# Hybrid encoder block: the softmax sums of the last four latent heads taken over by GpSimd additions

## The reference

```python
s = jnp.einsum('bqhd,bkhd->bhqk', q_blk, k).astype(jnp.float32) * scale
prob = jax.nn.softmax(s, axis=-1)
return jnp.einsum('bhqk,bkhd->bqhd', prob.astype(v.dtype), v)
```

## Time and profile before

| | us |
|---|---|
| median of 3 runs (lowest, highest) | 1581.14 (1579.66, 1581.53) |
| profiled execution: its own time | 1581.29 |
| its span in the profile | 1579.4 |
| PE busy | 1525.7 (97%) |
| DVE busy | 1051.0 (67%) |
| ACT busy | 636.6 (40%) |
| POOL busy | 349.3 (22%) |
| DMA, mean | 70 GB/s |

### The profile page before, as it was taken

How to read it: one execution, slowest core, us unless ns; L and a number is a source line. 1 busy time by engine, 2 the same in 40 slices (tenths; PEclk the granted TensorE clock), 3 DMA queues, 4 the chain that set the end, 5 groups by cost and what they waited for, 6 DMA issues and landing times.

```text
span 1579.4 us, 25838 instructions
## 1 busy us (share of the span) xinstructions
PE 1525.7 (97%) x10160; PEld 1104.2 (70%) x10160; DVE 1051.0 (67%) x1503; ACT 636.6 (40%) x1178; POOL 349.3 (22%) x356
## 2 busy tenths in 40 slices
PE   6999999999999999999999999999999999999998
PEld 5888776644555546777764457888888888888786
DVE  6424589678666676666548489875555555689877
ACT  5212247645444444444430125433333333343553
POOL 0810013146100028887830050220000000000000
PEclk9999999999999999999999999999999999999999
DMA  6141020010000000000033011333221111765322
GB/s 244 45 155 53 20 63 5 7 28 13 12 12 24 7 18 16 2 2 29 2 129 126 1 53 54 114 115 118 81 80 54 54 54 54 260 207 196 124 67 107
DMA packets 29001, 110.70 MB, mean 70 GB/s; under 512 B 3568, under 2 KB 6096, under 8 KB 26720
## 3 DMA queue, kind: packets, MB, share of 16 engines
q1 hardware_dynamic: 28432, 103.97, 19.5%
q0 software_dynamic: 464, 5.28, 0.8%
HBM read 89.36 MB, written 18.92 MB: 69 GB/s over the span
## 4 chain that ended last, share of the span: by engine, by line
PE 72%; issue 12%; DVE 9%; POOL 5%; ACT 2%; DMA 1%; DVEq 0%; SPq 0%; POOLq 0%; ACTq 0%
PE psum L2909 25%; PE psum L2926 12%; PE psum L2833 7%; PE psum L2579 4%; PE psum L2606 3%; PE psum L2497 2%; PE psum L2613 1%; PE psum L2516 1%; PE psum L2467 1%; POOL arena L853 1%; POOL arena L855 1%; PE psum L2807 1%; PE psum L2720 1%; PE psum L2716 1%; PE psum L2702 1%
## 5 line engine op out<-in xcount | busy, mean ns | idle before, releaser
L1988 DVE TENSOR_TENSOR part_lo<-arena,part_hi 128x512 fp32r<-128x512 f32 x154 | 117.7, 768 | 77.2 <-ACT part_hi L1269 77.0
L2909 PE MATMUL psum<-h_hi,part_hi 128*128 128x512 f32 x616 | 165.7, 391 | 1.1 <-ACT arena L1317 0.7
L2909 PE MATMUL psum<-h_lo,part_hi 128*128 128x512 f32 x616 | 164.7, 389 | 0.0
L2909 PE MATMUL psum<-h_hi,part_lo 128*128 128x512 f32 x616 | 164.7, 389 | 0.0
L1269 ACT ACTIVATE part_hi<-arena 128x512 fp32r<-128x512 f32 x154 | 95.9, 628 | 133.3 <-PE psum L2909 114.8
L2909 PEld LDWEIGHTS psum<-h_hi,part_hi 128*128 128x128 f32 x616 | 115.2, 188 | 26.7 <-ACT arena L1317 1.1
L2909 PEld LDWEIGHTS psum<-h_lo,part_hi 128*128 128x128 f32 x616 | 115.6, 188 | 24.1
L2909 PEld LDWEIGHTS psum<-h_hi,part_lo 128*128 128x128 f32 x616 | 115.6, 188 | 24.0
L919 POOL TENSOR_TENSOR arena<-arena,consts 128x512 f32<-128x512 f32 x64 | 81.8, 1299 | 179.9 <-ACT arena L1170 179.3
L1658 DVE TENSOR_REDUCE stats<-psum 128x1 f32<-128x1024 f32 x64 | 77.8, 1216 | 51.1 <-PE psum L2497 51.0
L2833 PE MATMUL psum<-arena 128*128 128x512 f32 x256 | 110.5, 592 | 0.0
(11 more groups left out here) (329 smaller groups left out, 3046.7 us busy)
## 6 DMA issues: line engine op xcount, KB each, us to landing
arena<-in_w_gate SPq DMA_DIRECT2D x22, 512.0 KB, 3.7
arena<-in_w_up SPq DMA_DIRECT2D x22, 512.0 KB, 3.8
arena<-in_w_down SPq DMA_DIRECT2D x22, 512.0 KB, 3.7
arena<-in_w_down SPq DMA_DIRECT2D x11, 1024.0 KB, 4.9
arena<-in_w_in SPq DMA_DIRECT2D x15, 512.0 KB, 3.5
arena<-act_spill SPq DMA_DIRECT2D x12, 512.0 KB, 7.1
act_spill<-arena SPq DMA_DIRECT2D x10, 512.0 KB, 6.1
arena<-in_x SPq DMA_DIRECT2D x8, 512.0 KB, 8.5
```

Of the source, the lines that this page charges most:

```text
L1988: v.tensor_tensor(lo, raw[:, at:at + HALF], hi, ALU.subtract).then_inc(part_lo, 1)
L2909: mm = pe.matmul(bank({2: z, 3: y, 5: y}.get(p, x)), w[:, P * k:P * k + P], h[k // 2][:, HALF * (k % 2):HALF * (k % 2) + HALF], start=(fre ...
```

## The change

For heads 4 to 7, GpSimd adds the exponentials of the key tiles into one of two buffers, tile by tile: 7 additions of 128x1024 for heads 4, 5 and 6, and 5 for head 7. TensorE then sums that buffer with 4 matmuls against ones (`sums_of`), which for heads 4 to 6 stand behind the first scores of the next head and for head 7 behind the second job A. Head 7's last two tiles are still summed by TensorE from the ring. ScalarE now also waits for `summed` before it reuses a ring buffer, and VectorE's `invert` of heads 4 to 6 waits for the scores behind `sums_of` instead of `pv_done`. GpSimd's chains for `Bt` and `Kt` begin one per head (`s_done` of 1, 9, 17, 25). The identity's DMA is issued behind four tiles of x. The loops over pairs on ScalarE and VectorE, and TensorE's third pass, are written out.

```diff
@@ sync
             for t in range(4):
                 sp.dma_start(resid[:, t, :], a["x"][t]).then_inc(rows_in_place[t], 16)
-                if t == 0:
-                    sp.dma_start(ident, a["consts"][:, 0:P]).then_inc(ident_in, 16)
+            sp.dma_start(ident, a["consts"][:, 0:P]).then_inc(ident_in, 16)
@@ gpsimd
-            pool.wait_ge(s_done, 1)
             for q in range(4):
                 hp = q % 2
+                pool.wait_ge(s_done, 8 * q + 1)
...
+            pool.wait_ge(kb_ready, 4)
+            for n in range(HEADS - SUMMED):
+                total = e_sums[n % 2]
+                for kt in range(1, NT if n < HEADS - SUMMED - 1 else NT - 2):
+                    pool.wait_ge(e_ready, 8 * (SUMMED + n) + kt + 1)
+                    if kt > 1:
+                        pool.wait_ge(summed, 7 * n + kt - 1)
+                    pool.tensor_tensor(total, e_ring[0] if kt == 1 else total, e_ring[kt % NE], ALU.add).then_inc(summed, 1)
@@ scalar, head_exps
+                    if add_up and (kt >= NE or first_summed < 2 * i + b):
+                        n = 2 * i + b - first_summed
+                        act.wait_ge(summed, 7 * n + max(kt - NE, 1) if kt >= NE else 7 * (n - 1) + kt + NE)
@@ vector, invert
-                v.wait_ge(pv_done, 8 * i + (4 * b + 4))
+                if add_up and 2 * i + b < HEADS - 1:
+                    v.wait_ge(s_done, 8 * (2 * i + b + 1) + 2)
+                else:
+                    v.wait_ge(pv_done, 8 * i + (4 * b + 4))
@@ tensor
+            def sums_of(i, b):
+                last = 2 * i + b == HEADS - 1
+                pe.wait_ge(summed, 7 * (2 * i + b - SUMMED + 1) - 2 * last)
+                pe.wait_ge(inverted, 2 * i + (b + 2))
+                for g in range(4):
+                    mm = pe.matmul(bank(7, 256, slice(32 * g, 32 * g + 32)), cst(C_ONES)[:, 0:32],
+                                   e_sums[b][:, 256 * g:256 * g + 256], start=True, stop=not last, skip_group_check=True)
...
-                for kt in (first, first + 1):
+                for kt in () if add_up and (i, b, first) != (HEADS // 2 - 1, 1, 6) else (first, first + 1):
                     for g in range(4):
...
                 scores(i, b, 0, ahead)
+                if left_over is not None:
+                    sums_of(*left_over)
                 scores(i, b, 1, ahead)
...
                 if not ahead:
                     pe.wait_ge(e_ready, 8 * HEADS)
                     attention(PLAN[1])
-                values(i, b, 6)
+                    sums_of(i, b)
+                values(i, b, 6, add_up)
```

More of the change, by code:

```diff
@@ L1171, in copy_attention, with head_exps @@
                                ACT.Copy, scale=-1.0).then_inc(out_a, 1)
-            def head_exps(i, b, ahead, ahead2, with_decays=False, last=False):
+            def head_exps(i, b, ahead, ahead2, with_decays=False, last=False, add_up=False):
+                first_summed = SUMMED
                 for kt in range(NT):
@@ L1208, in _ @@
                 head_exps(0, b, True, True, with_decays=True)
-            with act.Fori(0, HEADS // 2 - 2) as j:
+            for i in range(1, HEADS // 2 - 1):
                 for b in range(2):
-                    head_exps(j + 1, b, True, True)
+                    head_exps(i, b, True, True, add_up=2 * i >= SUMMED)
             for b in range(2):
-                head_exps(HEADS // 2 - 1, b, b == 0, False, last=True)
+                head_exps(HEADS // 2 - 1, b, b == 0, False, last=True, add_up=True)
             act.wait_ge(y_cleared, 5)
@@ L1816, in _ @@
             pair(0, None)
[L1817 to L1820, removed]
+            for i in range(1, HEADS // 2 - 1):
+                pair(i, i - 1)
             pair(HEADS // 2 - 1, HEADS // 2 - 2, last=True)
@@ L1825, in _ @@
                 if n == 2:
-                    invert(HEADS // 2 - 1, 1, last=True)
+                    invert(HEADS // 2 - 1, 1, last=True, add_up=True)
                 if job in DVE_AT:
@@ L2605, in values @@
                             rows = slice(64 * hf + 32 * c, 64 * hf + 32 * c + 32)
[L2606 to L2609 removed]
+                            mm = pe.matmul(bank(6, rows=rows), vh[b][:, kt, 32 * c:32 * c + 32],
+                                           e_ring[kt % NE][:, hf * HALF:(hf + 1) * HALF],
+                                           start=(kt == 0), stop=(kt == NT - 1), skip_group_check=True)
+                if first == 0 and not add_up:
                     pe.wait_ge(inverted, 2 * i + (b + 2))
[L2611 removed]
+                for kt in () if add_up and (i, b, first) != (HEADS // 2 - 1, 1, 6) else (first, first + 1):
                     for g in range(4):
@@ L2616, in values, with head @@
                 mm.then_inc(pv_done, 1)
-            def head(i, b, ahead, ahead2):
+            def head(i, b, ahead, ahead2, add_up=False, left_over=None):
                 nxt = (i + (b + 1) // 2, (b + 1) % 2)
@@ L2632, in head @@
                 ahead_guard(2)
-                values(i, b, 0)
+                values(i, b, 0, add_up)
                 ahead_guard(3)
@@ L2637, in head @@
                 ahead_guard(4)
-                values(i, b, 2)
+                values(i, b, 2, add_up)
                 ahead_guard(5)
@@ L2646, in head @@
                     attention(PLAN[0])
-                values(i, b, 4)
+                values(i, b, 4, add_up)
                 if ahead:
@@ L2668, in _ @@
             pe.wait_ge(z_sig, 14)
-            with pe.Fori(0, HEADS // 2 - 1) as i:
+            with pe.Fori(0, SUMMED // 2) as i:
                 for b in range(2):
                     head(i, b, True, True)
-            for b in range(2):
-                head(HEADS // 2 - 1, b, b == 0, False)
+            for h in range(SUMMED, HEADS):
+                before = ((h - 1) // 2, (h - 1) % 2) if h > SUMMED else None
+                head(h // 2, h % 2, h < HEADS - 1, h < HEADS - 2, add_up=True, left_over=before)
             for job in PLAN[2:]:
```

15 lines of the change are left out of this document (8 added, 7 removed).

## The result

The changed kernel takes 1581.67 us in the median of 20 runs (1580.63 to 1587.22), the kernel before 1579.84 (1576.72 to 1582.95, 20 runs beside it). The ratio is 1.002, interval [1.0012, 1.0027]: slower by 2 to 4 us. With 20 runs a side that can be told from no change, which the forecast had thought possible only from 3.2 us on. The forecast was 1579.0 and no change that can be told; the range held the time, the sign came out on the other side.

The account below looks back on a forecast made before the run. Bounds: TensorE in steady heads, late VectorE maxima in head 1, then the recurrence. Terms -0.2-5.4-7.8+11.3 = -2.1 against 1581.29 gave 1579.2, less 0.15 to the median 1579.0; own range 1575.5 to 1583, with rivals 1567.5 to 1586.

Parts of the forecast that it names:

- What bounds the kernel: TensorE in a steady head, late VectorE row maxima in head 1, the recurrence's chain through all engines from 584.10.
- The lock: A VectorE instruction with both inputs in SBUF waits for GpSimd's whole instruction, and the reverse; PSUM reads aren't held.
- Start: Step 1: the second tile of x comes sooner without 64 KB ahead of it; gain 0.2 us.
- The bound of 0.4: Bounds of 0 and 0.4 us on how much sooner the second tile of x comes at the start.
- Chains: Step 2: chains for `Bt` and `Kt` spread over heads free head 1 of lock waits; gain 5.4 us.
- Sums in heads 4 to 6: Step 3: fewer TensorE matmuls for softmax sums in these heads, additions taken at 2.0 us; gain 7.8 us together.
- the other end: An addition at 2.38 us, as the chains' products take; guards wait 0.7 in each of three heads, head 7 loses 13.1.
- the prediction's own signs of being wrong: Among them: L1643 gets longer than 3.2 us in heads 2 to 6 and guard 4 waits for it.
- Head 7: Step 4: additions and a late inversion delay VectorE's recurrence operands, G begins 10.8 us later; loss 11.3 us.
- The 0.5 for the clock and the second G: Added to head 7's loss for TensorE's clock falling after idleness and for the second direction's G: 0.5 us.
- Loops written out: Step 5: writing out the loops over pairs changes nothing.
- rival of 1585.8: Head 7 costs more than all heads gain, by additions of 2.38 and a clock staying low: 1585.8 us, chance 0.14.

Follow-up runs that it names:

- chains_only: The kernel before with one wait changed, so that GpSimd's chain for q waits for the first scores of head q: 1572.74 us.
- Experiments 4 to 6: head7_direct with GpSimd's third addition delayed (4), also the scaling behind the last row maximum (5), also head 6's sums before head 7's scores (6): 1567.19, 1563.35, 1560.72 us.
- head7_direct: The changed kernel with GpSimd's additions for heads 4, 5 and 6 only, head 7's sums made from the ring as before: 1568.93 us.
- experiment 9: The kernel before with two unused additions on GpSimd in head 7: 1579.89 us.
- experiments 3, 8 and 9: Three kernels with GpSimd additions in head 7: locked_head7, best_plus_head7 and experiment 9; 1589.98, 1571.35 and 1579.89 us.
- the last kernel: The last of Experiments 4 to 6 with GpSimd's sums for heads 2 to 6 and chains 2 and 3 cut into single operations: 1556.77 us.
- locked_head7: The kernel before with five unused additions on GpSimd in head 7: 1589.98 us.
- best_plus_head7: The last of Experiments 4 to 6 with head 7's five additions put back: 1571.35 us.
- head7_direct_yield: head7_direct with the third addition of heads 4 to 6 waiting for VectorE's subtraction of the turned queries: 1567.19 us.
- scale_behind: head7_direct_yield with VectorE's scaling of a pair of heads moved behind the last row maximum: 1563.35 us.

## Why the prediction was wrong

**What bounds the kernel** was read rightly but for one thing: in a steady head TensorE also waits 0.26 us for the guard behind VectorE's scaling. The lock was read rightly too, and every mechanism that the prediction named appeared where it was put. What failed were sizes: the gains of the start and of the chains came out larger than forecast, the gain of heads 4 to 6 half as large, and the loss in head 7 larger.

1. **Start**, forecast -0.2: about -2, by runs that say 0.2 to 3.3. The bound of 0.4 came from bandwidth alone, 64 KB less to move. The row that the step itself cited, a wait of 1.94 us for the second tile, vanished whole. The upper bound had to be that wait.
2. **Chains**, -5.4: -7.6 by the two traces, -6.5 by the runs of chains_only; I take 7. The step left head 1's guards 1.05 us of waiting; the longest wait is 0.35. That the clock need not fall was right, but what that gives was not in its sum for head 2: head 2 gained 2.9, of which 0.9 are waits and the rest goes with a granted clock of 1.00 instead of 0.95.
3. **Sums in heads 4 to 6**, -7.8: -3.8. **This is the step that failed.** It chose 2.0 us for an addition, "for it is the same operation and shape" as L855, and kept the chains' 2.38 as the other end. The additions take 2.38 in the median and 2.49 from one to the next. With 2.38 the step had reckoned the third addition's end at 11.9 us into the head and the maximum's at 14.2; in the trace they are at 11.88 and 14.21. Only the guard's waits came out at 1.12, 0.88 and 0.89 instead of 0.7, together 2.9 of the 4.0 us missing; where the step had allowed 0.3 for another guard, 0.16 stands. Experiments 4 to 6 show that the rest of the step was close: free of the lock the sums alone give about 7.6. One of the prediction's own signs of being wrong was there too: L1657, which was L1643, took 3.35 us in head 4, over its 3.2, and a guard waited for it.
4. **Head 7**, -11.3 in the other direction: +13.0, and +1.8 behind it. At 2.38 the step gives 13.1, but that this meets the 13.0 is partly luck: its turns at 2.38 would have cost 11 us and cost 10.0, while the inversion and the tiny products took 1.3 more than it said. Its order of events was right: inversion at 3.9 (3.5), five turns of about 2 us (10.0 in all, 9.15), the tiny products 2.2 (1.3), G at 36.8 (34.55). The 0.5 for the clock and the second G was too little: they cost 1.8 until GT.
5. **Loops written out**, nothing: chains_only keeps the loops and head7_direct has them written out, and their heads 1 and 2 agree within 0.03 us.

The sum with these values is -2-7-3.8+14.8 = +2. The prediction's own sum with the other end of its bound would have been -2.1+1.8+2.1 = +1.8: slower, as measured, though the size agrees by luck, since 3.4 us of unforeseen gain and as much of unforeseen loss cancel in it. Its rival of 1585.8 asked for 5.3 us beyond the sum; the additions' price, the guards and the clock together brought 7.5 in heads 4 to 7, and the start and the chains took 3.4 of them back.

The Trainium skill (GPSIMD Engine Reference, section 3.1) led to an estimate of 2.25 us for an addition; the trace has 2.38. It was nearer than the row I chose, and still short. On the lock, the Trainium skill ("SBUF — State Buffer", the section on two separate sides) says that whichever starts first keeps the shared pair for its whole instruction while the other fully blocks; the traces agree, with 1.87 us in experiment 9 for an operation of 128x8 elements that takes 0.17 alone. The traces add who is next: in all seventeen turns of head 7 in the changed kernel and experiments 3, 8 and 9, a waiting addition got in between two of VectorE's instructions, and a waiting VectorE instruction between two additions.

## What to carry to other kernels

Work on GpSimd is priced by what VectorE has in its queue then: cheap beside reads of PSUM (row maxima kept their 1.22 us beside additions, and heads 4 to 6 got 9% shorter), 1.6 to 2 us of VectorE's time for each instruction beside SBUF work, and that counts in full once VectorE's spare time is used up, by a wait moved later for instance. Put additions and chains where VectorE reads PSUM, and let GpSimd wait for the few SBUF operations that a critical engine waits for: four such edits turned a loss of 2 us into a gain of 18, and with two more heads 22. When two rows bound an unknown price, carry both ends to the sign of the sum before choosing one; the buffers and the place in the schedule were a better likeness than the operation's name.

## What the runs showed that I had not expected

- An addition of 128x1024 in place takes 2.00 us at L855 and 2.38 at L919, in the last kernel 2.36 to 2.40 in 35 of 35. The product just ahead of L855, on the same buffer, takes 2.40. What sets the two apart isn't settled: the operation, the shape and the type are the same, the places in memory are not. It wasn't tried.
- A small table ahead of a tile in a queue costs more than its bytes: 64 KB of identity, in rows of 512 bytes, delayed a tile of 512 KB by 2.0 to 2.6 us in four traces of five and by 0.6 in the fifth.
- TensorE's clock goes to half behind waits of 5.25 us (changed kernel) and 5.46 (locked_head7), 0.67 and 0.66 of full speed over a window of 10 us behind, and in best_plus_head7 to 0.66 behind waits of 3.34, 1.90 and 3.67. In head7_direct_yield and scale_behind it also fell around a wait of 1.41 us before head 7, while head7_direct (1.41) and the changed kernel (1.42) kept it; which of the two happens I can't tell from these traces.
